# Another order of ScalarE's and VectorE's work at the seams of a fused transformer kernel

## The reference

```python
# first block: layer 0 is a gated convolution, layer 1 an HGRN2 mixer
h = rms_norm(x, conv_norm);  x = x + conformer_conv(h, ...)   # 31 taps, layer norm, gate, w_out
h = rms_norm(x, hgrn_norm);  x = x + hgrn2_mixer(h, ...)      # 16 heads of 128, forward and backward, chunks of 64
# second block
h = rms_norm(x, g_mix)
... = split(h @ w_in)                     # NSA: q, k/v for compress, select, window, gates; GLA: q, k, v, a, r
x = x + concat([nsa, gla]) @ w_out        # 8 NSA heads, 4 GLA heads
hq = rms_norm(x, g_cross)                 # attention of 4 heads over a memory of 256 rows
x = x + softmax(cq ck^T) cv @ w_co
hf = rms_norm(x, g_ffn)
x = x + (silu(hf @ w_g) * (hf @ w_u)) @ w_down     # d_ff 5632
```

## Time and profile before

| What | Value |
|---|---|
| Median of 3 runs | 2431.47 us (2427.55 to 2434.13) |
| Profiled execution | 2434.97 us |
| Its span, first to last instruction | 2433.2 us |
| TensorE / its weight loads / VectorE / ScalarE / GpSimd busy | 2336.6 / 2067.9 / 1659.2 / 1281.1 / 226.7 us |
| Mean granted TensorE clock | 0.985 |

### The profile page before, as it was taken

How to read it: one execution, slowest core, us unless ns; L and a number is a source line. 1 busy time by engine, 2 the same in 40 slices (tenths; PEclk the granted TensorE clock), 3 DMA queues, 4 the chain that set the end, 5 groups by cost and what they waited for, 6 DMA issues and landing times. The chain is left out here.

```text
span 2433.2 us, 37832 instructions
## 1 busy us (share of the span) xinstructions
PE 2336.6 (96%) x14226; PEld 2067.9 (85%) x14226; DVE 1659.2 (68%) x2540; ACT 1281.1 (53%) x1444; POOL 226.7 (9%) x53
## 2 busy tenths in 40 slices
PE   6999999999999999999899888978999999999999
PEld 6999988888888888888788777867888888888888
DVE  6777776777877777767667566744666566655666
ACT  6556565666666566555566665454333333333343
POOL 4777720000000000000000000000000000000000
PEclk9999999999999999999999989999999999999999
DMA  5444444444434444556444322523555555555556
GB/s 223 174 174 174 174 162 167 173 156 159 171 138 158 153 155 149 188 216 225 139 144 156 132 87 104 186 108 116 178 184 182 189 188 190 180 186 187 189 191 223
DMA packets 57420, 409.25 MB, mean 168 GB/s; under 512 B 6496, under 2 KB 6624, under 8 KB 8544
## 3 DMA queue, kind: packets, MB, share of 16 engines
q1 hardware_dynamic: 57312, 407.82, 46.7%
HBM read 405.70 MB, written 2.10 MB: 168 GB/s over the span
## 5 line engine op out<-in xcount | busy, mean ns | idle before, releaser
L326 ACT ACTIVATE HI<-RAW 128x2048 fp32r<-128x2048 f32 x381 | 727.9, 1912 | 784.6 <-DMA RAW<-stream_dram 783.8
L333 DVE TENSOR_TENSOR LO<-RAW,HI 128x2048 fp32r<-128x2048 f32 x332 | 760.1, 2290 | 300.9 <-ACT HI L326 289.2
L350 PE MATMUL G<-HX,HI 128*128 128x512 f32 x1544 | 627.9, 407 | 13.1 <-DVE KN L1557 5.1
L349 PE MATMUL G<-HX,HI 128*128 128x512 f32 x1544 | 615.0, 398 | 0.0
L348 PE MATMUL G<-HX,LO 128*128 128x256 f32 x1544 | 432.9, 280 | 0.0
L351 PE MATMUL G<-HX,LO 128*128 128x256 f32 x1544 | 431.7, 280 | 0.0
L350 PE MATMUL G<-HXB,HI 128*128 128x512 f32 x992 | 394.2, 397 | 13.3 <-DVE HXB L2264 5.4
L349 PE MATMUL G<-HXB,HI 128*128 128x512 f32 x992 | 391.8, 395 | 0.0
L348 PEld LDWEIGHTS G<-HX,LO 128*128 128x128 f32 x1544 | 292.8, 190 | 71.1
L351 PEld LDWEIGHTS G<-HX,LO 128*128 128x128 f32 x1544 | 293.8, 190 | 64.1
L350 PEld LDWEIGHTS G<-HX,HI 128*128 128x128 f32 x1544 | 296.4, 192 | 19.6 <-issue 9.3
(11 more groups left out here) (356 smaller groups left out, 2672.0 us busy)
## 6 DMA issues: line engine op xcount, KB each, us to landing
RAW<-stream_dram SPq DMA_DIRECT2D x381, 1024.0 KB, 4.8
X<-x_dram SPq DMA_DIRECT2D x4, 512.0 KB, 5.1
MB<-mem_dram SPq DMA_DIRECT2D x4, 512.0 KB, 6.9
out_dram<-X SPq DMA_DIRECT2D x4, 512.0 KB, 7.7
CON<-constants_dram SPq DMA_DIRECT2D x1, 981.0 KB, 16.2
VEC<-vectors_dram SPq DMA_DIRECT2D x1, 623.5 KB, 17.2
VEC<-vectors_dram SPq DMA_DIRECT2D x1, 272.0 KB, 6.7
CON<-constants_dram SPq DMA_DIRECT2D x1, 64.5 KB, 1.9
```

Of the source, the lines that this page charges most:

```text
L326: nc.scalar.activation(HI[:, c.slot(RING), :], RAW[:, c.slot(RING), :], ACT.Copy).then_inc(hi_ready, 1)
L333: nc.vector.tensor_tensor(LO[:, c.slot(RING), :], RAW[:, c.slot(RING), :], HI[:, c.slot(RING), :].bitcast(F32), ALU.subtract).then_inc(lo_ ...
L349: return nc.tensor.matmul(res, wh, both[:, k, :, :], start=False, stop=last)
L350: nc.tensor.matmul(res, wh, both[:, k, :, :], start=first, stop=False)
```

## The change

It touches the queues at these places:

- `Norm.plan`: nine steps of chunk 0, the sums, the rest of chunk 0, then all of chunk 1 (before: 15 steps of each, the sums between them, then the last step of each).
- `Project.act`: in the first four tiles of a projection with `ahead` above 2 (conv_out) the feed stands in front of the split; the table of Ln is loaded ahead of the last feed, in every projection with a norm.
- hgrn: all 16 heads are written out on TensorE, ScalarE and VectorE; `keys` stands in front of `gate`, `values` in front of ZG's eviction; the lower bounds are computed aside in conv_out.
- mixa's tail runs inside mixb's head 0: on TensorE after chunk 0, on VectorE after chunk 0's eviction, with its four waits spread over the head; on ScalarE the HI split of chunk 2 goes ahead of the gates' sigmoid.
- cross: the two HX low parts each wait for their own high part; in CO two splits come first, low parts follow their own additions, and two splits of FF chunks stand between; the FF plan gives chunk 1 only 8 steps ahead of chunk 0's last four (before: 12).
- FF: `gated(k - 1)` stands in front of the first LO of `pair(k)`.

```diff
-            def plan(self, cut=KT - 1):
-
-                return [(0, 0, cut), self.sums, (1, 0, cut), (0, cut, KT), (1, cut, KT)]
+            def plan(self):
+
+                return [(0, 0, 9), self.sums, (0, 9, KT - 1), (0, KT - 1, KT), (1, 0, KT)]
...
+                        late = first and self.ahead > 2
+                        if self.n and late and j:
+                            feed(At(self.r0 + j - 1, 4, i), At(j - 1, 4, i))
                         if not (last and j + self.ahead > 5) and not (first and j < self.done):
                             split_hi(act, At(self.c0 + j + self.ahead, 4, i))
-                        if self.n and not (first and j == 0):
+                        if self.n and not late and not (first and j == 0):
                             feed(At(self.r0 + j - 1, 4, i), At(j - 1, 4, i))
...
                 if self.n:
+                    act.preload_act_table_set("natural_log")
                     feed(At(self.r0 + KT - 1), At(KT - 1))
...
-            for j in range(4):
+            for j in range(HEADS):
                 head(At(j), At(j - 1) if j else None)
-            with pe.Fori(1, 4) as i:
-                for j in range(4):
-                    head(At(j, 4, i), At(j - 1, 4, i))
...
                 if p:
+                    keys(p)
                     gate(p)
-                    keys(p)
...
                 if p:
+                    values(p)
                     wait(dve, hg_y, p)
                     result(p, 4, ZG[:])
                     mask(p)
-                    values(p)
                     both_ways(p)
...
+        def bounds_act(act):
+            act.wait_ge(s_rest, 32)
+            act.wait_ge(hg_lb, 2)
+            nc.scalar.activation(OML[:], OMN[:], ACT.Sigmoid).then_inc(hg_oml, 1)
+
+        def bounds_first(dve):
+            dve.wait_ge(s_rest, 32)
...
+        def bounds_last(dve):
+            dve.wait_ge(hg_oml, 1)
+            nc.vector.tensor_scalar(OMN[:], OML[:], -1.0, None, ALU.mult).then_inc(hg_oml, 1)
+
+        conv_out.aside = (None, bounds_act, bounds_first)
...
+            split_hi(act, At(C_MIXB + 2))
             was_scaled(act, mixa_scaled("gate"))
...
                 if p:
                     turn(p)
+                else:
+                    mixa_tail_pe(pe)
                 gemm(pe, mixb_chunk(j, 1), mixb_result(j, 1))
                 if p:
                     values(p, kvp)
+                else:
+                    pe.wait_ge(mx_gt, 2)
                 sum_q(j)
                 gemm(pe, mixb_chunk(j, 2), mixb_result(j, 2))
                 if p:
                     sum_o(p, j + 1)
+                else:
+                    pe.wait_ge(mx_kn, 5)
+                    pe.wait_ge(mx_vw, 2)
+                    pe.wait_ge(mx_vc, 1)
                 scores(j, kvh)
...
                 evict_scaled(dve, c, mixb_result(j, 0), QCN[:])
                 if p:
                     turned(p)
+                else:
+                    mixa_tail_dve(dve)
+                    split_lo(dve, c + 3)
                 split_lo(dve, c + 4)
...
+            split_hi(act, At(C_CO + 2))
+            split_hi(act, At(C_CO + 3))
             for cc in range(4):
-                split_hi(act, At(C_CO + cc + 2))
+                if cc == 3:
+                    act.preload_act_table_set("natural_log")
...
+                if cc < 2:
+                    split_hi(act, At(C_FF + cc))
...
-            dve.wait_ge(cr_hh, 2)
             for b in range(2):
+                dve.wait_ge(cr_hh, b + 1)
...
+            split_lo(dve, At(C_CO + 2))
+            split_lo(dve, At(C_CO + 3))
             for cc in range(4):
-                split_lo(dve, At(C_CO + cc + 2))
-                if cc:
-                    low(cc - 1)
                 wait(dve, mm_done, C_CO + cc + 1)
...
+                if 0 < cc < 3:
+                    split_lo(dve, At(C_FF + cc - 1))
+                low(cc)
...
-                    split_lo(dve, c + 2)
                     if not first:
                         gated(k - 1)
+                    split_lo(dve, c + 2)
```

More of the change, by code:

```diff
@@ L957, in build @@
         hg_zg = sem("hg_zg")
-        STEPS_ST = 15
         def order(d, s):
@@ L1127, in omn @@
                 return OMN[:, d, v:v + 1] if isinstance(v, int) else OMN[:, d, bass.ds(v, 1)]
-            act.wait_ge(hg_lb, 2)
-            nc.scalar.activation(OML[:], OMN[:], ACT.Sigmoid).then_inc(hg_oml, 1)
             act.wait_ge(hg_oml, 2)
-            for j in range(4):
+            for j in range(HEADS):
                 head(At(j), At(j - 1) if j else None, At(j - 2) if j > 1 else None)
-            with act.Fori(1, 4) as i:
-                for j in range(4):
-                    head(At(j, 4, i), At(j - 1, 4, i), At(j - 2, 4, i))
             last = At(HEADS - 1)
+            keys(last)
             gate(last)
-            keys(last)
             high(last - 1)
@@ L1271, in head @@
                     finish(p)
-            for d, n in enumerate(("lbf", "lbb")):
-                a0, a1 = V_AT[n + "0"], V_AT[n + "1"]
-                nc.vector.tensor_tensor(OMN[:, d, :], VEC[:, a0:a0 + HEADS], VEC[:, a1:a1 + HEADS], ALU.subtract).then_inc(hg_lb, 1)
-            dve.wait_ge(hg_oml, 1)
-            nc.vector.tensor_scalar(OMN[:], OML[:], -1.0, None, ALU.mult).then_inc(hg_oml, 1)
             st = Steps(dve, hg_stp)
-            for j in range(4):
+            for j in range(HEADS):
                 head(At(j), At(j - 1) if j else None, At(j - 2) if j > 1 else None, st)
-            with dve.Fori(1, 4) as i:
-                st2 = Steps(dve, hg_stp, 4 * STEPS_ST, i, st.n - 4 * STEPS_ST)
-                for j in range(4):
-                    head(At(j, 4, i), At(j - 1, 4, i), At(j - 2, 4, i), st2)
-                st2.end()
             last = At(HEADS - 1)
             wait(dve, hg_y, last)
+            values(last)
             result(last, 4, ZG[:])
             mask(last)
-            values(last)
             both_ways(last)
             gate(last)
-            states(last, Steps(dve, hg_stp, base=st.n + 3 * 4 * STEPS_ST))
+            states(last, st)
             low(last - 1)
@@ L1297, in hgrn_dve @@
             low(last)
+        def bounds_act(act):
[4 more added lines that the diff above has]
+            dve.wait_ge(s_rest, 32)
+            for d, n in enumerate(("lbf", "lbb")):
+                a0, a1 = V_AT[n + "0"], V_AT[n + "1"]
+                nc.vector.tensor_tensor(OMN[:, d, :], VEC[:, a0:a0 + HEADS], VEC[:, a1:a1 + HEADS], ALU.subtract).then_inc(hg_lb, 1)
+        def bounds_last(dve):
+            dve.wait_ge(hg_oml, 1)
+            nc.vector.tensor_scalar(OMN[:], OML[:], -1.0, None, ALU.mult).then_inc(hg_oml, 1)
+        conv_out.aside = (None, bounds_act, bounds_first)
         hgrn_out = Project(C_HGO, R_HGO, norm_mix, H_HGY, operand=HXB, feeds=HX, plan=[], done=1)
@@ L1419, in mixa_pe, with mixa_tail_pe @@
                                               start=True, stop=True).then_inc(mx_kss, 1)
+        def mixa_tail_pe(pe):
             pe.wait_ge(mx_hs, 2)
@@ L1541, in mixa_dve, with mixa_tail_dve @@
             evict_scaled(dve, mixa_chunk("gate"), mixa_result("gate"), AL[:])
+        def mixa_tail_dve(dve):
             dve.wait_ge(mx_c2, 2)
@@ L1669, in head @@
                 c = mixb_chunk(j, 0)
-                split_hi(act, c + 2)
+                if p:
+                    split_hi(act, c + 2)
                 split_hi(act, c + 3)
@@ L1738, in weigh @@
                 wait(dve, ns_e, j + 1)
+                dve.wait_ge(mx_gt, 3)
                 st.link(nc.vector.reciprocal(RC[:], SL[:]))
@@ L1753, in head @@
                     other(p, 3)
-                split_lo(dve, c + 3)
+                    split_lo(dve, c + 3)
                 wait(dve, ns_sqq, j)
@@ L1770, in head @@
                 st.end()
-            dve.wait_ge(mx_gt, 3)
             for kvh in range(2):
@@ L2177, in cross_pe @@
                     sums_x(cc - 1)
-            parts[0].plan = [(0, 0, 12), lambda pe: sums_x(3), (1, 0, 12), (0, 12, 16), (1, 12, 16)]
+            parts[0].plan = [(0, 0, 12), lambda pe: sums_x(3), (1, 0, 8), (0, 12, 16), (1, 8, 16)]
         def cross_act(act):
@@ L2274, in cross_dve @@
                     nc.vector.tensor_tensor(x, x, A[2 + 2 * (cc % 2) + b][:].rearrange("p (a t) -> p a t", a=2), ALU.add).then_inc(cr_x, 1)
-            low(3)
+                if 0 < cc < 3:
+                    split_lo(dve, At(C_FF + cc - 1))
+                low(cc)
         at = Layout(AFTER_HN)
@@ L2434, in _ @@
             conv_out.act(act)
-            act.wait_ge(s_rest, 32)
             hgrn_act(act)
@@ L2450, in _ @@
             conv_out.dve(dve)
-            dve.wait_ge(s_rest, 32)
+            bounds_last(dve)
             hgrn_dve(dve)
```

4 lines of the change are left out of this document (removed).

## The result

| | before | after |
|---|---|---|
| Median | 2429.56 us (4 runs, 2427.55 to 2434.13) | 2388.12 us (4 runs, 2387.57 to 2389.61) |
| Profiled execution, its span | 2434.97, 2433.2 | 2388.18, 2386.4 |
| Mean granted TensorE clock | 0.985 | 0.992 |

The ratio is 0.9828 (95% interval 0.9811 to 0.9845): 41.4 us on the medians, 46.8 between the two profiled executions. Forecast were 2386.5 and a sum of 45.9. The profiled execution of before is one of the longest of its kernel, of which 25 other executions took 2424.46 to 2435.01, so some 5 us of the 46.8 lie between executions and not between the kernels.

A forecast was written before the change was run, and what follows sets the result against it. TensorE, 96% busy, was taken as the bound, losing time in single waits at seams and half clock behind them. Terms summed to 45.9 us off 2434.97; adjusted to the median, plus 1 for eviction waits: 2386.5, range 2378 to 2399.

The forecast's parts named there:

- hgrn, 10.8: In hgrn, unrolling removes two backward branches of VectorE's loop, at 5.4 us each: 10.8 us, bounds 0 and 11.6.
- Rival (b): In hgrn, unrolling brings nothing because the 3.87 us idle is not the branch's: 2397 us, chance 7%.
- conv_out, 3.3: At conv_out's front, putting the feed first gains 3.8 us less 0.5 for the bounds: 3.3, bounds 1.5 and 3.8.
- The 0.5 for the bounds: In conv_out, the lower bounds' two new steps make the third addition end about 342.1 against 341.6: 0.5 us lost.
- Head 0, 5.1: In hgrn's first head, TensorE passes KD 3.4 us sooner and 1.7 of half clock goes: 5.1, bounds 3.4 and 6.4.
- the 2 us for the bounds: At hgrn's start, the lower bounds' table load with its wait cost ScalarE's path about 2 us.
- Mixa 0.6: In mixa, the new plan removes chunk 2's wait for its slot: 0.6 us.
- Cross 3.9: In cross, the fourth query square comes sooner (3.3 us) and HX low parts start per bank (0.65): 3.9 us.
- Mixer's tail, 7.5: In mixb's head 0, chunk 0 runs at once, the KN wait goes, none is late: 7.5 us, bounds 3.5 and 8.5.
- CO and FF, 10.8 + 3.2 + 0.7: CO to FF's second chunk gains 10.8, the FU wait 3.2, FF's second part 0.7: 14.7 us, bounds 7 and 18.
- The term of 3.2: In FF, evicting FU ahead of the LO removes TensorE's 3.0 us wait, 3.2 with its tail.

The follow-up runs named there:

- run 4: Changed kernel, hgrn still written out, with gate and ZG's eviction ahead of keys and values again and Ln's early table loads removed: 2387.87 us.
- run 1: Changed kernel with hgrn's heads 4 to 15 back in engine loops on TensorE, ScalarE and VectorE: 2388.25 us.
- run 8: Changed kernel with the split again before the feed in conv_out, and FF's first LO again before gated(k - 1): 2393.66 us.
- run 7: Changed kernel with the lower bounds computed at hgrn's start again instead of aside in conv_out: 2386.49 us.
- run 6: Changed kernel with Norm.plan as before, 15 steps of each of the two chunks with the sums between: 2397.75 us.
- run 10: Changed kernel with the mixer's tail ahead of mixb's head 0 again on TensorE, VectorE and ScalarE: 2394.10 us.
- run 9: Changed kernel with CO's splits, copies and low parts in the old order, FF's plan of 12 steps, no preload in CO: 2396.57 us.
- run 11: Changed kernel plus a gla reordering: sums, kv and the next gate run inside a head's second chunk, VectorE's order adapted: 2372.39 us.
- run 5: Changed kernel with hgrn's loops back on all three engines, keys still first, but values after ZG's eviction, result and mask: 2388.70 us.
- run 3: Changed kernel with hgrn's loops back on all three engines and gate and ZG's eviction ahead of keys and values again: 2394.47 us.
- run 2: Changed kernel with hgrn's heads 4 to 15 in a loop on TensorE and ScalarE only, VectorE's written out: 2388.79 us.

## Why the prediction was right or wrong

The size was right: 45.9 against 46.8 between the profiled executions, 2386.5 against a median of 2388.1. So was the view of the kernel, single waits at seams with half clock behind them, and the mechanism of steps 2, 3, 5 and 6 in the main. The nearness of the sum is in part luck: the stages that the terms speak of won 49.4, and 2.7 were lost in mixb's rest, gla and mix_out, where no edit aimed at anything. From before's median of then, 2431.47, the forecast was 45.0 down; by the medians of four it was 41.4. By steps:

1. **hgrn, 10.8: measured 5.35 + 5.57 = 10.92.** The chain is as told: the pause behind VectorE's branch, ZG, the sigmoid, KX. What failed is the last sentence of the step, "keys ahead of gate and values ahead of result hide under the same chunks: KX comes one table load sooner", which puts the new order at nothing. Behind the same split, KX starts 1.8 us after that split's start in after and 5.7 us in run 4 (old order, no loops): it is 3.8 us sooner, since not only the load of 1.28 but also the wait of 2.12 for ZG and the sigmoid's 0.42 no longer stand in front of it. With that much in hand, the pause of 3.93 us reaches nobody (run 1). So the order takes the loss away alone (run 1), the unrolling takes it away alone (run 4), and their effects are not to be added; the prediction gave all of it to the unrolling. Rival (b), whose number was 2397, had the cause wrong, since the pause stands behind VectorE's branch in every kernel with VectorE's loop and in none without; yet its name, that unrolling brings nothing, is what run 1 shows in the new order. The Trainium skill (Runtime: NRT & Kernel Launch, Instruction fetch mechanics) says that a taken branch whose target is outside the two held pages stalls its engine; run 1 agrees by its 3.93 us, though no run shows where the target lay. The same section of the Trainium skill prefers full unrolling for that reason: in the old order that agrees (2394.47 against 2387.87), in the new order it is worth nothing (2388.25 against 2388.12), since nobody waits for the stall.
2. **conv_out, 3.3: 3.32**, and 0.58 that no edit made. Run 8 brings back wait and half clock, 3.81. The 0.5 for the bounds was right as well (0.57, run 7).
3. **Head 0, 5.1: 5.49.** KD's wait is 1.2 as forecast and no half clock follows. But the plan alone carries 5.43 (run 6); the 2 us for the bounds, which the prediction put on ScalarE's path, are nothing (runs 6 and 7).
4. **Mixa 0.6: 2.10**, all of it the plan's (run 6). The term was mis-sized, since only the slot's wait of 0.59 was counted: two more, of 0.18 for LO and 0.63 for HN, go and come with it. **Cross 3.9: 1.24 + 2.96 = 4.20** from the stage's start to CO's first product. Run 6 takes back 1.24 + 2.37 = 3.61 of it. The wait for HX, now per bank, went from 2.10 to 1.50 us, in run 6 too, and that 0.60 is the rest; it was not tried by itself.
5. **Mixer's tail, 7.5: 8.07** in head 0. None of the four waits spread over the head is late. Undone it costs 8.63 there, and 6.0 on the median (run 10). The 0.75 that mixb's rest lost is within what executions of the same code differ by.
6. **CO and FF, 10.8 + 3.2 + 0.7: 10.86 + 3.14 + 0.68.** The first is counted as in the prediction, from CO's first product to the end of FF's second chunk, 52.32 us before and 41.46 after; the second is FF's next two chunks. Of the first, 1.51 lies in CO's first chunk (in the table under attention and CO), where before runs 3.41 us at half clock at 1642.80 and after does not. The prediction had left that stretch in, so its 41.5 was hit although this 1.7 went: the other parts were as much too short. No run shows an edit that removed the stretch. It stays away with CO's old order (run 9) and with the old plan (run 6), and it is back in run 11 behind the same wait of 1.50 for HX. CO's order is 8.9 (run 9), gated's place 1.7 instead of 3.2 (run 8). The term of 3.2 was read from a wait that two causes made together: 2.97 us without both edits, 1.51 with CO's alone (run 8), none with gated's alone (run 9). The 0.68 of the second part is there in run 8 as well, so it is not of that edit; what it is of stays open.

Not foreseen: gla is 1.59 longer. Its waits are as before within 0.5 us in sum, half clock lies over 23.9 us of it instead of 20.5, and in run 5's execution the same code is 1.42 shorter again.

The medians of the runs that undo a part sum to 9.6 + 8.5 + 6.4 + 6.0 + 5.5 = 36.0 (bounds -1.6 left out) of 41.4. Of the 5.4 between, a candidate is the 4.4 by which heads 8 and 12 lost more in before's profiled execution (10.92, with 6.83 us of half clock behind each wait) than in run 3's (6.52). Whether before's other executions lose that much there is not shown.

## What to carry to other kernels

A stall of an engine off the critical path costs only through the instruction that the critical engine's operand is queued behind: before you remove the stall, ask whether that operand can be moved in front of what waits. When two edits each cut the same chain, only the four kernels of the square (both, either, none) tell what each is worth. And look last at the stages that a change leaves alone: most of the waiting left after it, but for the kernel's start, stood in gla and attention, and in gla the same kind of reordering brought 15.7 us more.

## What the runs showed of the hardware

- A taken backward branch over VectorE's four heads (some 340 recorded instructions) is recorded with 55 to 63 ns and followed by 3.67 to 3.97 us without work (runs 1, 3 and 5; before, with 3.87 in the earlier trace rows and 3.97 the second time); the loop's exit and ScalarE's and TensorE's branches over the same heads show no such pause.
- The same wait does not always bring the same half clock: behind 2.60 us for KX in head 12, run 3 runs at 1.00, and before, behind 2.58, at 0.50 for 6.83 us. What decides it was not found. In gla the same code took 98.13 us with 20.5 us at half clock (run 5), 99.55 with 23.9 (after) and 99.90 with 27.3 (run 2).
- A chunk's period is 5.65 us in conv_out, hgrn_out and FF, but in some executions 5.60 over a whole stretch, at the same granted clock of 1.00: after's has it in conv_out, runs 4 and 10 in hgrn_out, run 9's in hgrn_out and FF, and that execution is 4 us shorter than its kernel's median. In a stage's difference of some tenths this has to be taken off first. No view says why.
- In hgrn's roots Ln and Exp each have a load of 1.28 us in front of them. An early load of Ln's table moves one of the two off the chain as long as no other function comes between (run 7 has it a second time behind the bounds' sigmoid), and run 4 shows that this was worth nothing here.
